# The convolved feed-forward's first projection with 512 moving columns, and its convolution taps made from a sum in SBUF

## The reference, cut to what matters

```python
D_FF = 2816
CONV_WIDTH = 3

def conv_ffn(h, w_up, conv_w, conv_b, w_down):
    s = h.shape[1]
    u = h @ w_up                                   # (256, 1024) @ (1024, 5632)
    up = jnp.pad(u, ((0, 0), (CONV_WIDTH - 1, 0), (0, 0)))
    u = conv_b + sum(conv_w[j] * up[:, j:j + s] for j in range(CONV_WIDTH))
    gate, val = u[..., :D_FF], u[..., D_FF:]
    return (jax.nn.silu(gate) * val) @ w_down
```

## Time and profile before

| | us |
|---|---|
| median of 3 runs | 1009.71 (1009.64 to 1009.95) |
| the profiled execution, its own time | 1009.63 |
| its span, first to last instruction | 1007.8 |
| PE busy | 998.1 (99%) |
| PE weight loads busy | 911.5 (90%) |
| DVE busy | 703.2 (70%) |
| ACT busy | 590.7 (59%) |

### The profile page before, as it was taken

How to read it: one execution, slowest core, us unless ns; L and a number is a source line. 1 busy time by engine, 2 the same in 40 slices (tenths; PEclk the granted TensorE clock), 3 DMA queues, 4 the chain that set the end, 5 groups by cost and what they waited for, 6 DMA issues and landing times.

```text
span 1007.8 us, 17093 instructions
## 1 busy us (share of the span) xinstructions
PE 998.1 (99%) x6928; PEld 911.5 (90%) x6928; DVE 703.2 (70%) x1179; ACT 590.7 (59%) x987; POOL 0.4 (0%) x5
## 2 busy tenths in 40 slices
PE   9999999999999999999999999999999999999997
PEld 7899999999999999999999888888999899888886
DVE  4698888878888676887658665655766558565652
ACT  4778665557555556767647545554666547455453
POOL 0000000000000000000000000000000000000000
PEclk9999999999999999999999999999999999999999
DMA  9965667535667545453326556455553326555521
GB/s 384 358 245 190 257 233 293 196 148 210 232 256 263 192 162 187 173 209 126 126 88 219 201 203 206 169 183 201 209 189 139 127 105 251 198 178 176 205 80 42
DMA packets 28013, 196.76 MB, mean 195 GB/s; under 512 B 3104, under 2 KB 3744, under 8 KB 4640
## 3 DMA queue, kind: packets, MB, share of 16 engines
q1 hardware_dynamic: 27360, 194.95, 53.3%
q10 hardware_dynamic: 576, 0.72, 0.2%
HBM read 194.61 MB, written 1.05 MB: 194 GB/s over the span
## 4 chain that ended last, share of the span: by engine, by line
PE 96%; ACT 1%; DVE 1%; issue 0%; ACTq 0%; POOLq 0%
PE PS L1011 11%; PE PS L1012 11%; PE PS L1013 11%; PE PS L1195 10%; PE PS L1286 8%; PE PS L1287 8%; PE PS L1288 8%; PE PS L1198 5%; PE PS L1165 3%; PE PS L1168 3%; PE PS L1166 3%; PE PS L1228 2%; PE PS L1230 2%; PE PS L1229 2%; PE PS L1383 2%; PE PS L1372 1%
## 5 line engine op out<-in xcount | busy, mean ns | idle before, releaser
L1830 DVE TENSOR_TENSOR wlo<-raw,whi 128x1024 fp32r<-128x1024 f32 (+1 forms) x314 | 368.2, 1217 | 76.6 <-ACT whi L1448 73.9
L1448 ACT ACTIVATE whi<-raw 128x1024 fp32r<-128x1024 f32 x308 | 306.7, 1047 | 61.8 <-PE PS L1288 55.0
L1011 PE MATMUL PS<-HX,whi 128*128 128x256 f32 x816 | 234.9, 288 | 1.3 <-DVE HX L1804 1.3
L1012 PE MATMUL PS<-HX,whi 128*128 128x256 f32 x816 | 230.8, 283 | 0.0
L1013 PE MATMUL PS<-HX,wlo 128*128 128x256 f32 x816 | 230.7, 283 | 0.0
L1011 PEld LDWEIGHTS PS<-HX,whi 128*128 128x128 f32 x816 | 156.3, 191 | 7.8 <-issue 7.0
L1012 PEld LDWEIGHTS PS<-HX,whi 128*128 128x128 f32 x816 | 156.4, 192 | 0.5
L1013 PEld LDWEIGHTS PS<-HX,wlo 128*128 128x128 f32 x816 | 156.3, 192 | 0.0
L1195 PE MATMUL PS<-HX,whi 128*128 128x512 f32 x416 | 147.9, 398 | 0.0
L1286 PE MATMUL PS<-whi,Oh 128*128 128x512 f32 x344 | 134.6, 391 | 0.0
L1287 PE MATMUL PS<-wlo,Oh 128*128 128x512 f32 x344 | 134.2, 390 | 0.0
(11 more groups left out here) (262 smaller groups left out, 1600.2 us busy)
## 6 DMA issues: line engine op xcount, KB each, us to landing
raw<-wall SPq DMA_DIRECT2D x155, 1024.0 KB, 4.9
raw<-wada SPq DMA_DIRECT2D x18, 1024.0 KB, 5.1
GA<-wada SPq DMA_DIRECT2D x2, 1024.0 KB, 18.2
GA<-alibi SPq DMA_DIRECT2D x1, 2048.0 KB, 9.3
raw<-wall SPq DMA_DIRECT2D x2, 768.0 KB, 5.7
X<-xt SPq DMA_DIRECT2D x1, 1024.0 KB, 5.2
KM<-wada SPq DMA_DIRECT2D x1, 1024.0 KB, 13.2
QF<-wada SPq DMA_DIRECT2D x1, 1024.0 KB, 16.6
```

The source lines that it names most:

```text
L1011: e.matmul(dst, wh, a, start=start, stop=False, skip_group_check=share)
L1012: e.matmul(dst, wh, b, start=False, stop=False, skip_group_check=share)
L1448: e.activation(whi[place(n)][:, c], raw[i % RAW][:, c], ACT.Copy).then_inc(*up("a_whi", (n, half)))
L1830: e.tensor_tensor(wlo[place(n)][:, c], raw[i % RAW][:, c], f32(whi[place(n)][:, c]), ALU.subtract).then_inc(*up("v_wlo", (n, half)))
```

## The change

U2 to U21 use `wide` instead of `rows`: per k-tile and output tile one matmul of 512 columns and one of 256 in place of three of 256. The results lie in two adjacent banks, the part from the low inputs in each bank's second half. ACT copies both second halves to a region of `PT` (new `ev_up_wide`), DVE adds the first halves to them there, and both the first tap (ACT) and the other two (DVE) read this sum in SBUF (new `up_taps`). `up_gate` of the chunk before stands between the sum and the taps. Both banks are free when DVE has written the sum. The region in `PT` is single, so ACT's copy for Uj waits for DVE's last tap of U(j-1). `st["at"] += st["at"] % 2` makes the pairs start at an even bank. `final_squares`, which uses the same region of `PT` after the last chunk, waits for the taps of U21.

```diff
     def ev_up(n, b, j):
-        emit("ev_up", n, b, j)
+        emit("ev_up_wide", n, b, j)
         while pending:
             emit("up_gate", pending.pop(0))
+        emit("up_taps", j)
...
             together([("up", 0), ("up", 1)], "ffn", ev_first)
+
+            st["at"] += st["at"] % 2
             pending.append(1)
         else:
-            rows(("up", 2 * i), "ffn", evac=lambda n, b, pr, j=2 * i: ev_up(n, b, j))
+            wide(("up", 2 * i), "ffn", lambda n, b, j=2 * i: ev_up(n, b, j))
...
-            rows(("up", 2 * i + 1), "ffn", evac=ev_second)
+            wide(("up", 2 * i + 1), "ffn", ev_second)
...
+            elif step == "ev_up_wide":
+                free[a[1]] = free[a[1] + 1] = ("v_u", ("up", a[2], "sum"))
...
             elif step == "final_squares":
                 i, = a
                 on.wait_ge("v_u2", (19, 19, 19, 20)[i])
+                on.wait_ge("v_u", ("up", 21))
...
+            elif step == "ev_up_wide":
+                n, b, j = a
+                on.wait_ge("t_mm", (n, 1))
+                on.wait_ge("v_u", ("up", j - 1))
+                e.activation(PTf[:, 1024:1536].rearrange("p (j t) -> p j t", j=2), PS[:, b:b + 2, T:2 * T], ACT.Copy).then_inc(
+                    *up("a_part", n))
+            elif step == "up_taps":
+                j, = a
+                on.wait_ge("v_u", ("up", j, "sum"))
+                if j >= 3:
+                    on.wait_ge("v_u2", j - 3)
+                for i, tile in enumerate((j, 22 + j)):
+                    m = e.activation(
+                        PBf[:, (j % 3) * 512 + i * T:(j % 3) * 512 + i * T + T], PTf[:, 1024 + i * T:1280 + i * T],
+                        ACT.Identity, bias=col("conv_b", tile), scale=col("conv_w", 88 + tile))
+                m.then_inc(*up("a_u", ("up", j)))
...
+            elif step == "ev_up_wide":
+                n, b, j = a
+                s = PTf[:, 1024:1536].rearrange("p (j t) -> p j t", j=2)
+                on.wait_ge("a_part", n)
+                e.tensor_tensor(s, PS[:, b:b + 2, 0:T], s, ALU.add).then_inc(*up("v_u", ("up", j, "sum")))
+            elif step == "up_taps":
+                j, = a
+                on.wait_ge("a_u", ("up", j))
+                for tap, sh in ((1, 1), (0, 2)):
+                    for i, tile in enumerate((j, 22 + j)):
+                        u = PBf[:, (j % 3) * 512 + i * T + sh:(j % 3) * 512 + i * T + T]
+                        if tap == 0:
+                            on.wait_ge("v_u", ("up", j, "first"))
+                        m = e.scalar_tensor_tensor(
+                            u, PTf[:, 1024 + i * T:1280 + i * T - sh], col("conv_w", tap * 44 + tile), u, ALU.mult, ALU.add)
+                    m.then_inc(*up("v_u", ("up", j, "first") if tap else ("up", j)))
```

More of the change, by code:

```diff
@@ L504, in stages, with ev_second @@
             together([("up", 0), ("up", 1)], "ffn", ev_first)
+            st["at"] += st["at"] % 2
             pending.append(1)
         else:
-            rows(("up", 2 * i), "ffn", evac=lambda n, b, pr, j=2 * i: ev_up(n, b, j))
+            wide(("up", 2 * i), "ffn", lambda n, b, j=2 * i: ev_up(n, b, j))
             pending.append(2 * i)
-            def ev_second(n, b, pr, j=2 * i + 1):
+            def ev_second(n, b, j=2 * i + 1):
                 ev_up(n, b, j)
```

## The result

| | before | after |
|---|---|---|
| median of 6 runs, us | 1009.64 (1009.14 to 1009.95) | 1014.58 (1013.97 to 1015.88) |
| profiled execution, us | 1009.63 | 1014.23 |
| its span, us | 1007.8 | 1012.4 |
| ratio, 95% interval | | 1.0048 [1.0038, 1.0058] |

A forecast was written before the change was run, and what follows sets the result against it. TensorE bounds the stage, with DVE a second chain of nearly equal length. U14 2.60 us late less 0.93 from the other 8 wide chunks is +1.67 on 1009.63: 1011.3 us, range 1010.0 to 1014.6.

The forecast's parts named there:

- likeliest case: Whole kernel: DVE chain of about 6.45 us a chunk and no fall of the clock, 1011.3 us; chance 0.60.
- the clock falls in the wait: TensorE's mid-kernel stop of 3.9 us lowers its clock, costing 2.7 us more: 1014.0 us; chance 0.25.
- Wide chunks: TensorE, U2 to U21: 5.640 us a chunk against 5.756, 0.116 less each, 2.32 us for 20.
- The DVE cycle from the bounds of single rows: DVE, one U chunk from sum to sum: 6.45 us against 5.82, with bounds 6.2 and 6.55.
- U12's sum: DVE, after the ada pieces: reaches this sum at 323.83 us and has it at 324.57.
- The wait: TensorE before the ACC transposes: stands still 3.9 us, 320.69 to 324.57, for the banks of U12's pair.
- The single region: PT: ACT's copy waits for the last tap before it, about 2.2 us before DVE wants it, costing nothing.
- the matmuls gain nothing: TensorE in this stage: wide chunks stay at 5.756 us, only the DVE wait is left, 1012.2 us; chance 0.02.
- DVE keeps up: DVE cycle under 6.06 us leaves no wait, 1007.3 us; chance 0.08 for DVE cheaper, down to this.
- its chain is longer: DVE: later ACT copy or tap costs 1.1 us per tenth in the cycle; 6.65 gives 1013.5 us; chance 0.05.
- One of about a tenth ahead of U14: TensorE before U14: a second wait of about a tenth, ready at 330.91, U13's sum ready at 331.02.
- DVE catches up and TensorE does not wait again: After ada: DVE needs 15.18 us per pair and D chunk, TensorE 16.75, so no further waits.

The follow-up runs named there:

- its own run: Changed kernel with two regions for the half sums used in turn, order of steps unchanged: 1014.93 us, ratio 1.0051.
- 1.6 us did not lower the clock: Changed kernel with the second ada piece of the fifth group cut to one column of ACC, so DVE arrives earlier: 1010.33 us, ratio 1.0004.
- the wait of 5.8: Changed kernel with ACT and DVE steps reordered (weight split fills the hand-over waits), the sum keeping its single region: 1018.55 us, ratio 1.0087.
- 2.4 with 4.3: Kernel before with one added wait: transposes after U13 wait for DVE's low part of hidden values of chunk 12: 1016.17 us, ratio 1.0063.
- 2.8 with 3.1: Kernel before with one added wait: transposes after U13 wait until DVE's taps of U13 are done: 1013.82 us, ratio 1.0044.
- the run without the stop: Changed kernel with the ada sum of column block 5, and so TensorE's ACC transposes, moved from after U13 to after U19: 1011.55 us, ratio 1.0015.
- the fastest kernel: Changed kernel with ACT and DVE steps reordered, two regions for the sum, and U21 back in its narrow form: 1007.76 us, ratio 0.9982.
- run 16: Not a follow-up run: the words belong to "TensorE had just run 16 or 20 matmuls of a single column each"; no measured time.
- the reordered kernel: Changed kernel with ACT and DVE steps reordered so the weight split fills DVE's waits, and two regions for the sum: 1008.78 us, ratio 0.9988.

## Why the prediction was right, and where it was short

The range (1010.0 to 1014.6) holds the median of 1014.58 by 0.02 us, which is luck: three of the six executions lie above it. The likeliest case (1011.3) is 3.3 us too low. What happened is the rival "the clock falls in the wait", which the prediction priced at 1014.0 and gave a chance of 0.25.

**Right, with its sizes.** Wide chunks 5.64 forecast, 5.645 measured. The DVE cycle from the bounds of single rows: 6.45 forecast, 6.47 measured, made as forecast of 0.60, 0.45 and 0.32 up to the taps, an idle of 0.56 for ACT's tap, and taps from SBUF no cheaper (1.79 for four, where the earlier trace rows have 1.77). U12's sum: start forecast at 323.83, measured 323.48, in an execution that was 0.5 ahead. The wait: 3.9 and 3.9, released by DVE's sum of U12 (the trace names L2278 and gives 3.74 of idle time, as it lets the last matmul's end run on). The single region: no cost, shown by its own run. These rows exclude the rivals in which the matmuls gain nothing, DVE keeps up or its chain is longer.

**The step that failed: the choice between the two cases of the clock.** The trace before has no wait over 0.5 us in mid-kernel, so it could not decide; I took the case without a fall as the likelier. The traces show: 1.6 us did not lower the clock in the profiled execution, 3.1 did in its profiled execution but in one other did not, and in the profiled executions with 3.8 to 5.8 it fell each time. The size, 2.7 forecast and 2.59 measured, is right in part by luck. The rows of the opening burst give rather 2.4 (52 matmuls at 2.40 for 20 are 6.24 us, not the 6.0 that I used), and what such a fall costs is no constant: over the 6.34 us from the transposes to U14 it was 1.7 with the wait of 5.8, 2.4 with 4.3, 2.6 here, 2.8 with 3.1, and 2.9 with 3.8 in the kernel with two regions alone (334.42 - 325.16 = 9.26). In each it is about half of the time from the end of the wait to the clock's rise. The Trainium skill (page "TensorE: Matmul & The Clock Gate", section "HAM oscillation — how this bites in real kernels") was right against my choice here: idle stretches dropped the clock, and the time was that rival's. The figure of the Trainium skill for an isolated start (same page, section "Back-to-back issue gap"), by which the gain would be 0.8 us in all (an estimate), does not hold here: 12 chunks alone gave 1.3.

**"One of about a tenth ahead of U14".** Not there. It was to come from U14 ready at 330.91 and U13's sum at 331.02. With TensorE at half pace U14 was ready only at 333.24, and the sum long there (329.94 + 0.69 = 330.63). At the upper clock U14 would have been ready at 324.31 + 6.34 = 330.65, so even then next to nothing would have been left of it.

**"DVE catches up and TensorE does not wait again".** Right in its first half, short in its second. DVE does gain the 16.75 - 15.18 = 1.6 us on each pair and D chunk. But I looked for waits up to D10's matmuls, and left out ACT's copy behind U21's chain, which held TensorE up by 0.5 us although it had stood still for 3.9 and run at half pace for 5.4. In the run without the stop this wait was 2.2, the larger part of it (by the estimate above) DVE's reductions of `ACC`, which I had not counted where they now stood. Because of this the time without the wait (1007.5 to 1008.2 expected, 1011.55 measured) was wrong too.

**A small one.** D chunks that follow wide chunks take 5.503 us against 5.468 before, 0.28 us in all eight; the later layer's D chunk in the earlier trace rows, 5.47, had been taken for them. Why it is longer here no run shows.

## What to carry to other kernels

Where a second engine's cycle is within some per cent of TensorE's, add up its new cycle hand-over by hand-over before looking at the matmuls, and follow its lag to every later place where a buffer or an accumulator is asked for, the end of the layer included. When a step is moved, look at what moves with it on the other engines: here the transposes took 1.6 us of DVE's work along. Price a TensorE wait like those here, of 3.1 us and more, with the clock's loss on top (1.7 to 2.9 us). Fill a hand-over wait with work that needs neither side (here the weight split), and check for each reordering what stands behind the instruction that now waits.

## What the runs showed of the hardware that I had not expected

- The clock's answer to a wait is not the same in each execution: the identical kernel with a 3.1 us wait took 1012.73 us at a mean clock of 0.999, which is the wait alone, and 1016.38 at 0.993 in the execution whose trace shows the fall in the wait (2.8 us) and another near 55.
- The clock can also fall while TensorE waits for nothing. In the profiled execution of the fastest kernel it is at half level in the opening, where TensorE does 17 matmuls in three microseconds (26 in the same window of the kernel before):

```profile
11.00:14.00 3.00, 3.00 (x17) 2.03 (x10) 0.00 (x0) 0.00 (x0) 0.00 (x0) 0.50 0.99 418
```

- Four of the twelve traces have such a stretch: the two reordered kernels with two regions from 10.7 to 14.1, the two kernels with an added wait from about 55.4 to 58.8. In all four TensorE had just run 16 or 20 matmuls of a single column each (L1020 of the kernel before). The eight other executions ran the same ones and kept the clock. The four have one more thing in common: in them the opening burst went fastest, its 52 matmuls taking 7.5 us up to the next matmul, against 8.0 to 8.8 in the eight others. What ties the two together no run shows.
- One such stretch costs 1.7 us, half its length; in the opening a part of it is made up for by the burst before, which was at least 0.5 us shorter. The executions of one kernel are spread by 1 to 1.5 us (1007.65 to 1009.21 in the reordered kernel), as much as the whole gain that the change can bring. Such stretches are a likely reason, but of the executions that were not profiled only the mean clock is known. A difference under 1 us needed some ten runs of each kernel and, better, distances inside the traces.
